# Twelve blocks transposed by DMA instead of TensorE in a three-stage decoder layer

## The reference

```python
x = x + rmsnorm(parallel_conv_mixer(rmsnorm(x, mix_pre_g), ...), mix_post_g)
x = x + rmsnorm(memory_cross_attention(rmsnorm(x, xa_pre_g), mem_n, ...), xa_post_g)
x = x + rmsnorm(swiglu_ffn(rmsnorm(x, ffn_pre_g), w_gate, w_up, w_down), ffn_post_g)

# mixer: h (S, 1024) -> 2560 columns: B, C, v (head group A), GLU value, GLU gate (head group B)
y_a = b_a * causal_dwconv3(c_a * v_a)
y_b = silu(layernorm(causal_dwconv31(glu_v * sigmoid(glu_g)) + bias))
mix = concat([y_a, y_b]) @ w_mix_out
# attention: 4 heads of 256 over 256 fixed memory tokens; FFN: hidden width 2816
ffn = (silu(h @ w_gate) * (h @ w_up)) @ w_down
```

## Time and profile before

| what | us |
|---|---|
| median of 3 runs (lowest, highest) | 889.1 (887.85, 889.79) |
| the profiled execution | 889.61 |
| span of its slowest core (core 7) | 887.0 |
| spans of the other cores | 884.3 to 886.4 |
| TensorE (PE) busy in that span | 849.1 (96%) |
| VectorE (DVE), ScalarE (ACT), GpSimd (POOL) busy | 390.0, 298.3, 125.9 |

### The profile page before, as it was taken

The page is one execution under the profiler, slowest core; times in us unless marked ns, Lnnn a source line. Parts: engine busy times, 40 slices in busy tenths (PEclk is TensorE's granted clock), DMA queues, the critical chain, the costliest instruction groups (busy, mean ns, idle before and its releaser), DMA issues.

```text
span 886.4 us, 13126 instructions; the slowest of 8 cores (884.3 to 887.0 us)
## 1 busy us (share of the span) xinstructions
PE 849.1 (96%) x4795; PEld 432.8 (49%) x4872; DVE 390.0 (44%) x500; ACT 298.3 (34%) x544; POOL 125.9 (14%) x290
## 2 busy tenths in 40 slices
PE   2899999999999899999999999999999999999997
PEld 1657444555664455554444444444444444444443
DVE  1477758437547678886522122331232322221122
ACT  2332345532636668765331111221122211111111
POOL 3121113112103132321110010000000000000000
PEclk9999999999999999999999999999999999999999
DMA  9599057368894257877696012122121121210011
GB/s 195 153 179 192 1 185 253 124 128 139 168 221 91 50 148 188 190 153 184 194 182 118 1 72 95 37 60 72 72 95 36 48 84 72 67 53 1 1 48 71
DMA packets 33327, 97.94 MB, mean 110 GB/s; under 512 B 11344, under 2 KB 11472, under 8 KB 32368
## 3 DMA queue, kind: packets, MB, share of 16 engines
q0 software_dynamic: 7344, 33.03, 23.4%
q1 hardware_dynamic: 25920, 64.07, 21.5%
HBM read 107.05 MB, written 20.97 MB: 144 GB/s over the span
## 4 chain that ended last, share of the span: by engine, by line
PE 92%; ACT 3%; issue 2%; DMA 1%; DVE 1%; DVEq 0%; SPq 0%; POOL 0%; POOLq 0%; ACTq 0%
PE pp L374 89%; PE pp L433 3%; ACT t L354 3%; DMA t<-x 1%; DVE t L1003 1%; DVE t L367 0%; ACT L354 0%; DVEq L1193 0%; SPq L377 0%; DVE t L371 0%; POOLq L1193 0%; ACT pp L354 0%; POOL t L357 0%; ACTq L187 0%; POOL t L363 0%
## 5 line engine op out<-in xcount | busy, mean ns | idle before, releaser
L374 PE MATMUL pp<-t,t 128*128 128x512 bf16 (+2 forms) x4195 | 819.2, 354 | 7.9 <-ACT t L354 2.7
L374 PEld LDWEIGHTS pp<-t,t 128*128 128x128 bf16 x4272 | 397.0, 98 | 411.2 <-issue 6.9
L357 DVE TENSOR_TENSOR t<-pp,t 128x512 bf16<-128x512 f32 (+4 forms) x173 | 150.4, 873 | 365.8 <-PE pp L374 194.7
L354 ACT ACTIVATE t<-pp 128x512 f32<-128x512 f32 (+5 forms) x208 | 153.3, 750 | 355.8 <-PE pp L374 336.6
L367 DVE SCALAR_TENSOR_TENSOR t<-t,t,t 128x1024 bf16<-128x1024 f32 (+4 forms) x100 | 126.5, 1271 | 49.3 <-POOL t L357 29.7
L361 POOL TENSOR_SCALAR t<-t 128x1 f32<-128x1 f32 (+2 forms) x102 | 24.7, 242 | 627.5 <-ACT t L354 323.3
L433 PE MATMUL pp<-t,t 128*128 128x128 bf16 (+1 forms) x600 | 43.2, 222 | 23.0 <-DVE t L367 19.8
L354 ACT ACTIVATE pp<-pp 128x1024 f32<-128x1024 f32 (+1 forms) x17 | 16.3, 958 | 142.4 <-PE pp L374 142.4
L357 POOL TENSOR_TENSOR t<-t,t 128x1 f32<-128x1 f32 (+2 forms) x103 | 60.7, 589 | 15.6 <-POOL t L361 0.6
L354 ACT ACTIVATE t<-pp,t 128x256 bf16<-128x256 f32 (+2 forms) x76 | 43.9, 583 | 42.8 <-DVE t L1003 34.2
L354 ACT ACTIVATE t<-t 128x1024 bf16<-128x1024 f32 (+2 forms) x52 | 53.9, 1037 | 8.7 <-DMA t<-x 8.7
(11 more groups left out here) (26 smaller groups left out, 65.2 us busy)
## 6 DMA issues: line engine op xcount, KB each, us to landing
t<-x SPq DMA_DIRECT2D x68, 512.0 KB, 6.7
x<-t SPq DMA_DIRECT2D x24, 512.0 KB, 3.6
t<-w_gu POOLq DMA_DIRECT2D x22, 512.0 KB, 6.8
out<-t SPq DMA_DIRECT2D x15, 512.0 KB, 2.8
t<-w_dn POOLq DMA_DIRECT2D x6, 768.0 KB, 20.2
t<-gains SPq DMA_DIRECT2D x6, 512.0 KB, 9.4
t<-w_ing POOLq DMA_DIRECT2D x8, 256.0 KB, 16.5
t<-w_inc POOLq DMA_DIRECT2D x4, 512.0 KB, 10.4
```

The costliest lines, as they stand in the source:

```text
L354: S.op("act", lambda e: e.activation(out=out, in_=in_, func=func, **kw), reads, writes)
L357: S.op(eng, lambda e: e.tensor_tensor(out=out, in0=in0, in1=in1, op=op), reads, writes)
L374: S.op("pe", lambda e: e.matmul(out, lhsT=lhsT, rhs=rhs, start=start, stop=stop), reads, writes, signal)
```

## The change

The blocks of the mixer's second tile (eight) and of the FFN's second tile (four) are transposed by `dmaT` right after their DVE step, in place of `t8`. The requests for the down weights move from slices 3 to 9 of the first FFN tile to slices 7 to 12, and the load of the gain `G4` from slice 12 to 14.

```diff
+        def td_x(b, hs):
+            dmaT("hxT%d" % (b % 4), hT[:, :, b * 128:(b + 1) * 128], hst[hs], ["hs%d" % hs], ["h%d" % b])
+
         def pn2(b):
             hp[b] = px2(pt1[b], xn[b])
+            td_x(b, hp[b])
...
             if b in (3, 5, 7):
                 pn2(b // 2 - 1)
-            if b in (6, 7):
-                t_x(b - 6, hp[b - 6], "act")
...
             if b + 3 < 8:
                 hp[b + 3] = px2(pt1[b + 3], xn[b + 3])
+                td_x(b + 3, hp[b + 3])
             glu_ev(b, *g)
-            if b + 2 < 8:
-                t_x(b + 2, hp[b + 2], "act")
...
-        WDL = {3: [(0, 4)], 4: [(4, 3)], 5: [(7, 3)], 6: [(10, 3)], 7: [(13, 3)], 8: [(16, 3)], 9: [(19, 3)]}
+        WDL = {7: [(0, 4)], 8: [(4, 3), (7, 3)], 9: [(10, 3)], 10: [(13, 3)], 11: [(16, 3)], 12: [(19, 3)]}
...
-                    if jj - 2 in p3 and t == 0:
-                        t_3(4 + p3.index(jj - 2), hs3, "act")
                     if jj in p3:
                         k = p3.index(jj)
                         hs3 = prep3((t + 1) * 4 + k)
-                        if t > 0:
-                            dmaT("h3T%d" % k, h3[(t + 1) % 2][:, :, k * 128:(k + 1) * 128], hst[hs3], ["hs%d" % hs3],
-                                 ["g%d_%d" % ((t + 1) % 2, k)])
+                        dmaT("h3T%d" % k, h3[(t + 1) % 2][:, :, k * 128:(k + 1) * 128], hst[hs3], ["hs%d" % hs3],
+                             ["g%d_%d" % ((t + 1) % 2, k)])
...
-                if t == 0 and jj == 12:
+                if t == 0 and jj == 14:
                     dma("sp", "G4", G4[:], gain_d[GN_FFPOST], [], ["G4"])
```

## The result

The changed kernel takes 891.43 us (median of 13 runs), the kernel before 888.84 beside it: a ratio of 1.0029 with a 95% interval of 1.0021 to 1.0037, so 2.6 us slower (1.9 to 3.3). The forecast was 887.8 us, in a range of 884.0 to 891.2. All ratios here leave out executions that a slower state of the chip disturbed; the medians do not.

What follows compares the result with a forecast made beforehand. Bound by PE's chain, matmuls being 89% of the span. Saving 3.56 us (mixer) and 1.78 (FFN) against a 4.0 us stall gave -1.3, so 889.1 became 887.8 us, range 884.0 to 891.2.

Steps and rivals of the forecast that it cites:

- The mixer's and the FFN's groups: Twelve groups of PE transposes removed, 0.445 us each: 3.56 us in the mixer and 1.78 in the FFN.
- one wait at `glu(3)`: Fourth GLU product of the second mixer tile: PE waits 2 to 5 us for block 3's DMA transpose.
- rival C: Mixer queue: a transpose costs only its bytes as a copy, 0.68 us; stall 1.9, time 885.7 us; chance 0.1.
- their shift, which I had called free: First FFN tile: requesting the down weights later costs nothing, with some 3 us of cover before the first down product.
- Block 5's load: Mixer's out stage: delayed by block 2's transpose, it lands near 155, in time for ACT's square after 154.9.
- a stall of 4.0 us: PE's wait at `glu(3)`: 3.2 us from the queue plus 0.8 for a moderately late landing.
- 158.0 + 2 x 1.17 + 1.17 = 161.5: Landing of block 3's transpose: last store's old landing, plus blocks 1 and 2's transposes, plus its own time.
- 0.8 on top: Added to the 3.2 us stall at `glu(3)` for one moderately late landing, because the slowest of eight cores counts.
- the forecast's 158.3: Start of `glu(3)` without a stall: 160.51 less 2.23 us for five groups of transposes removed ahead of it.
- the price of the five copies: Queue in front of block 3's transpose: three loads and two stores at 1.36 us each, 6.8 us together.
- Nothing behind takes the stall back: After `glu(3)`: PE works without a gap up to 186, then waits for work that follows PE itself.
- Rival D: Mixer queue: each transpose delays copies behind it 1.5 us more; stall 9.1, time 892.9 us; chance 0.2.

Runs made afterwards that it cites:

- `ffn_only`: The change's FFN half alone, with all mixer blocks transposed by TensorE as in the kernel before: 887.1 us, ratio 0.998.
- `ffn_wd_early`: The change's FFN half alone, mixer by TensorE, but down weights requested at slices 3 to 9 as before the change: 894.74 us, ratio 1.0065.
- `t12_pe`: The changed kernel with the mixer's blocks 1 and 2 transposed by TensorE again: 888.72 us, ratio 0.9995.
- the filler's second run: The changed kernel plus 16 idle matmuls in front of the fourth GLU product, run again beside the changed kernel: 892.33 us, ratio 1.0032.
- `six_blocks`: The changed kernel with only the mixer's blocks 2 and 3 transposed by TensorE again, FFN half as in the change: 884.79 us, ratio 0.995.
- `block3_pe`: The changed kernel with only the mixer's block 3 transposed by TensorE again: 887.33 us, ratio 0.9984.

## Why the prediction was wrong

**What held.** The mixer's and the FFN's groups are worth 5.34 us together: `ffn_only` measures the FFN's share, 1.8 against 1.78. The place of the loss, one wait at `glu(3)`, its cause, a transpose behind the stage's last copies in SP's queue, and the order of the issues held. So did the price of a transpose in the queue: block 3's landed 1.1 us behind the last store on all eight cores (1.17 forecast; rival C had 0.68). The down weights arrived in time; `ffn_wd_early` shows that their shift, which I had called free, was also necessary. Block 5's load, of which I had said that it would be in time, was not: ACT waited 3.8 us for it, under the cover of the longer wait.

```profile
158.28 1.06 ACT L354 ACTIVATE t<-t 128x1024 bf16<-128x1024 f32 x1 [3.82 <-DMA t<-x]
```

**The term that was mis-sized.** The sum had a stall of 4.0 us, from "158.0 + 2 x 1.17 + 1.17 = 161.5" and 0.8 on top. It was 5.7 in the mean and 7.0 on the slowest core. On core 0 PE came to the product 0.9 us earlier than the forecast's 158.3, and the block landed 2.8 later than its 161.5: 3.2 + 0.9 + 2.8 is 6.9 of the 7.0 us of the wait.

The step that failed is the price of the five copies. They had been given 1.36 us each, 6.8 together, from the stretch 151.2 to 158.0 of core 7. Core 7 was the fastest there: on the other seven cores of the same execution the same five transfers, from the landing of the store ahead of them to that of the last store, took 7.6 to 9.5 us, 8.3 in the mean. The two stores on core 4 of the kernel before:

```profile
L377 SPq DMA_DIRECT2D x<-t x1: 319/319/319, 145.0 to 145.0; - x1
DMA to landing us min/median/max: 3.3/3.3/3.3
...
L377 SPq DMA_DIRECT2D x<-t x1: 326/326/326, 152.0 to 152.0; - x1
DMA to landing us min/median/max: 5.9/5.9/5.9
```

From 148.3 to 157.9, 9.5 us. In the changed kernel the five take 8.2 to 9.8 us from the landing of block 2's transpose, 9.1 in the mean, 2.3 more than the forecast. On core 0 that transpose landed at 148.74 + 4.9 = 153.6; the first load and the last store behind it:

```profile
L377 SPq DMA_DIRECT2D t<-x x1: 570/570/570, 150.0 to 150.0; - x1
DMA to landing us min/median/max: 8.1/8.1/8.1
...
L377 SPq DMA_DIRECT2D x<-t x1: 965/965/965, 152.6 to 152.6; - x1
DMA to landing us min/median/max: 10.6/10.6/10.6
```

So they landed from 158.1 to 163.2: the first copy took 4.5 us, the other four 1.2 to 1.3 each, the forecast's price and a little less. From 153 to 162 the queue moved 61, 184, 193, 197, 274, 406, 434, 414 and 362 GB/s: slow at first, then at its best rate. On seven of the eight cores the first copy behind block 2's transpose took 2.4 to 4.7 us. A slow copy of this kind was there before the change too, with no transpose in this stretch: one of 2.2 to 3.6 us among the five on each of the cores 0 to 6, and none on core 7, where the rate fell earlier, to 107 and 66 GB/s near 149. I had taken the one core whose five copies had missed it. `t12_pe` agrees that the copies are the slow part. Why one of them is slow there, whether all eight cores ask for memory at once or a load suffers behind a store, no run here separates; it stays open.

**The term that was missing.** "Nothing behind takes the stall back" left out that the stall costs more than itself. The clock was at half for 10 us around the end of the wait on core 0, and the 112 matmuls behind it took 27.23 us on core 0 and 26.0 on core 3, against 24.33 at the full clock: 2.9 and 1.7, some 2.0 in the mean of the cores. No case of the forecast had this.

**The balance.** Means of the cores: -5.34 + 5.7 + 2.0 = +2.4 us, measured +2.6. For core 0: -5.34 + 7.0 + 2.9 = +4.6, while its span rose from 884.4 to 890.8; the other 1.8 lie ahead of the wait: PE was through with block 6's out-projection at 143.6 (157.42, the start of the wait, less four products of 3.45) and at 141.7 in the execution before (145.58, the start of block 1's PE transposes there, less a step of 3.90). Most of it is not the change's: a group of matmuls of the first mixer tile, which both kernels share, starts at 31.77 in one execution and at 30.23 in the other. Rival D named the right side and the right place, and set the turning point correctly at 5.34 us of stall, but its mechanism, that a transpose holds the copies behind it for 1.5 us beyond its own time, is not shown: without the two transposes the landing moved by 2.5 us, and 2.3 are their own time. A smaller hold isn't excluded, since the five copies took 9.1 us in the mean behind them and 7.9 in `t12_pe`. D's 892.9 is nearest to the measured time partly by luck, as its 9.1 us of stall had no clock in it: the stall was 5.7 and the clock added 2.0.

## What to carry to other kernels

Moving a transpose from TensorE to a DMA exchanges a fixed 0.45 us for a landing time that depends on the whole queue: do it for blocks that are issued when the queue has nearly drained (blocks 4 to 7 and the FFN's, 884.7 us, better than both kernels), leave the others where they are, and move bulk loads out of the stretch. Price a queue by its slow stretches and by all cores, not by its best rate on one; here the trace of the kernel before had the right order of size (8.3 us for five copies in place of 6.8) on seven cores. Price a TensorE wait with the slower matmuls behind it: here 5.7 us of wait cost 7.7.

## What the runs showed of the hardware that was not expected

- A DMA transpose behind copies landed in the order of issue in SP's queue, and late among the weights of POOL's: 2.8 us to landing alone, 10.6 behind five copies, 18.6 to 39 among the down weights. SP's own issue of it took 1.22 us, but 5.4 with a full queue and 14.4 among the weights, and whatever SP had next waited too.
- After PE had stood for 2.7 us (157.4 to 160.1) the granted clock went to half; it came back at 170.3, 5.9 us after PE had resumed. The length of the wait alone doesn't tell. In the filler's second run the matmuls ran at the full clock behind waits of 2.3 to 3.2 us on four cores, but slower behind one of 3.0. In `six_blocks` they ran at the full clock behind 3.0, while in `block3_pe` core 5 took 22.57 us for the 96 matmuls behind a wait of 1.99, where 20.88 is the full rate.
- Behind a full queue a DMA transpose of 262 KB took 1.1 us and each of the last two copies of 524 KB in front of it 1.2 to 1.3 us (changed kernel, all cores, from landing to landing); single copies ahead of these took up to 4.7 us.
